# A fp32 two-block transformer stack on one core: taking the filler matmuls out of the norm transposes

## What is computed

```python
def swiglu(x, w_gate, w_up, w_down):
    return (jax.nn.silu(x @ w_gate) * (x @ w_up)) @ w_down
...
# first block, for layer in range(2)
f = swiglu(rms_norm(h, ffn1_pre_g[layer]), ...)
h = h + 0.5 * rms_norm(f, ffn1_post_g[layer])
hn = rms_norm(h, mix_pre_g[layer])
m = recurrent_block(hn, ...) if layer == 0 else forgetting_attention(hn, ...)
h = h + rms_norm(m, mix_post_g[layer])
f = swiglu(rms_norm(h, ffn2_pre_g[layer]), ...)
h = h + 0.5 * rms_norm(f, ffn2_post_g[layer])
...
# second block, for layer in range(4)
h = h + 0.5 * swiglu_2(rmsnorm(h, ffn_norm[layer, 0]), ...)
h = h + mix                              # gdn, short conv, nsa, gdn
h = h + 0.5 * swiglu_2(rmsnorm(h, ffn_norm[layer, 1]), ...)
```

## Time and profile before

| | |
|---|---|
| median of three runs | 3331.31 us |
| lowest and highest run | 3329.32 and 3336.26 us |
| the profiled execution, its own time | 3333.94 us |
| its span, first to last instruction | 3331.9 us |
| mean granted TensorE clock | 0.985 |
| TensorE (PE) busy | 3228.4 us, 97% |
| weight loads (PEld) busy | 2725.3 us, 82% |
| VectorE (DVE) busy | 1844.8 us, 55% |
| ScalarE (ACT) busy | 1561.7 us, 47% |
| DMA | 537 MB at 161 GB/s |

### The profile page before, as it was taken

One profiled execution on the slowest core, in us unless ns is written; L12 is line 12 of the kernel. 1 busy time (PEld: TensorE's weight loads), 2 busy tenths in 40 slices (PEclk: granted clock), 3 DMA queues, 4 the chain that ended last, 5 costly groups with the idle time before them and its releaser, 6 DMA issues.

```text
span 3331.9 us, 48269 instructions
## 1 busy us (share of the span) xinstructions
PE 3228.4 (97%) x18934; PEld 2725.3 (82%) x18934; DVE 1844.8 (55%) x2023; ACT 1561.7 (47%) x1896; POOL 187.4 (6%) x187
## 2 busy tenths in 40 slices
PE   7999999999999999989999999999999999999899
PEld 6878888887788889978888978888767888898787
DVE  4467556545545557555554655554655455475544
ACT  4446544444544446454454444444545444464543
POOL 0000001000000300300000000000410000003000
PEclk8999999999999999999999999999989999999999
DMA  7543554555255654225555555565513556551354
GB/s 228 189 149 121 183 189 159 182 186 168 95 189 164 193 186 153 78 91 192 187 184 189 169 164 186 173 195 189 158 52 114 185 173 197 177 159 60 115 188 139
DMA packets 415536, 537.14 MB, mean 161 GB/s; under 512 B 22956, under 2 KB 361084, under 8 KB 415152
## 3 DMA queue, kind: packets, MB, share of 16 engines
q1 hardware_dynamic: 413612, 528.76, 49.2%
q0 software_dynamic: 1792, 6.49, 0.8%
HBM read 534.13 MB, written 1.05 MB: 161 GB/s over the span
## 4 chain that ended last, share of the span: by engine, by line
PE 90%; DVE 4%; ACT 4%; DMA 1%; issue 1%; SPq 0%; ACTq 0%; DVEq 0%
PE banks L133 24%; PE banks L135 24%; PE banks L134 24%; PE banks L130 3%; PE banks L131 3%; PE banks L132 3%; PE banks L318 2%; PE banks L1891 1%; DVE w_lo L114 1%; ACT w_hi L106 1%; DMA raw<-ffn_w_up 1%; PE banks L253 1%; PE banks L1274 1%; PE banks L1003 1%; PE banks L1286 1%
## 5 line engine op out<-in xcount | busy, mean ns | idle before, releaser
L114 DVE TENSOR_TENSOR w_lo<-raw,w_hi 128x2048 fp32r<-128x2048 f32 x508 | 1169.6, 2307 | 663.6 <-ACT w_hi L106 663.5
L106 ACT ACTIVATE w_hi<-raw 128x2048 fp32r<-128x2048 f32 x508 | 970.6, 1916 | 509.5 <-PE banks L135 423.4
L133 PE MATMUL banks<-w_hi,xT_hi 128*128 128x512 f32 (+2 forms) x2588 | 1011.8, 391 | 38.8 <-DVE w_lo L114 14.6
L135 PE MATMUL banks<-w_hi,xT_lo 128*128 128x512 f32 (+2 forms) x2588 | 998.1, 386 | 0.0
L134 PE MATMUL banks<-w_lo,xT_hi 128*128 128x512 f32 (+2 forms) x2588 | 996.4, 385 | 0.0
L133 PEld LDWEIGHTS banks<-w_hi,xT_hi 128*128 128x128 f32 (+1 forms) x2588 | 491.1, 190 | 139.6 <-DVE w_lo L114 19.6
L135 PEld LDWEIGHTS banks<-w_hi,xT_lo 128*128 128x128 f32 (+1 forms) x2588 | 490.3, 189 | 98.0
L134 PEld LDWEIGHTS banks<-w_lo,xT_hi 128*128 128x128 f32 (+1 forms) x2588 | 491.4, 190 | 92.2
L133 PE MATMUL banks<-w_hi,hidT_hi 128*128 128x512 f32 x1056 | 411.9, 390 | 0.0
L135 PE MATMUL banks<-w_hi,hidT_lo 128*128 128x512 f32 x1056 | 411.1, 389 | 0.0
L134 PE MATMUL banks<-w_lo,hidT_hi 128*128 128x512 f32 x1056 | 410.9, 389 | 0.0
(11 more groups left out here) (431 smaller groups left out, 2423.5 us busy)
## 6 DMA issues: line engine op xcount, KB each, us to landing
raw<-ffn_w_gate_up SPq DMA_DIRECT2D x352, 512.0 KB
raw<-ffn_w_down SPq DMA_DIRECT2D x264, 512.0 KB
raw<-ffn_w_gate SPq DMA_DIRECT2D x88, 512.0 KB
raw<-ffn_w_up SPq DMA_DIRECT2D x88, 512.0 KB
raw<-gdn_w_in SPq DMA_DIRECT2D x64, 512.0 KB
raw<-sc_w_in SPq DMA_DIRECT2D x24, 512.0 KB
raw<-nsa_w_in SPq DMA_DIRECT2D x20, 512.0 KB
raw<-rg_w_in SPq DMA_DIRECT2D x20, 504.0 KB
```

The costliest lines, as they stand in the source:

```text
L106: c.nc.scalar.activation(c.w_hi[r][:], c.raw[r][:], ACT.Copy).then_inc(c.sem("w_hi_split"), 1)
L114: c.nc.vector.tensor_tensor(c.w_lo[r][:], c.raw[r][:], c.w_hi[r][:].bitcast(F32), ALU.subtract).then_inc(c.sem("w_lo_split"), 1)
L133: mm(out, x_hi, w_hi, start=start, stop=False)
L135: return mm(out, x_lo, w_hi, start=False, stop=stop)
```

## The change

The constant and the three lines of the loop are taken out. Nothing else differs: every other instruction of TensorE stands in the same order, and those of the other engines are the same. The bf16 identity and masks are still made at the start of the kernel and are used elsewhere.

```diff
@@ -233,7 +233,6 @@
         dve_rstd(c, dve, st)
 
 
-BUSY_MATMULS = 14
 
 
 def pe_norm(c, pe, st):
@@ -241,9 +240,6 @@
     if n == 0:
         pe.wait_ge(c.sem("masks_made"), MASK_STEPS)
     src = c.h if st.kind == "ffn" else c.xn
-    if n and (st.kind != "ffn" or st.source.post is not None and not st.keeps_h):
-        for _ in range(BUSY_MATMULS if st.source.post is None else 2 * BUSY_MATMULS):
-            c.nc.tensor.matmul(c.bank[NORM_BANKS[1]][:, 0:3 * P], c.ident_bf[:], c.causal_bf[:], start=True, stop=True)
     for m, t in PARTS:
         if st.kind == "ffn":
             wait_for_h(c, pe, st, m, t)
```

## The result

| | before | the change |
|---|---|---|
| median of nine runs | 3332.45 us | 3340.99 us |
| lowest and highest | 3328.98 and 3336.26 us | 3334.85 and 3344.24 us |
| ratio, 95% interval | | 1.0026 (1.0015 to 1.0036) |
| profiled execution, its time | 3333.94 us | 3339.73 us |
| its span, mean granted clock | 3331.9 us, 0.985 | 3337.2 us, 0.980 |

The change makes the kernel slower by 8.5 us, 5 to 12 by the interval. The time lies in my range; the size of the loss is 1.8 times my +4.7.

The account below looks back on a forecast made before the run. TensorE, busy for 97% of the span, was taken to bound the kernel. The terms 3.2 + 1.2 + 1.1 - 0.8 = +4.7 us on the 3331.3 us median gave 3336.0 us, range 3329.5 to 3343.0.

Parts of the forecast that it names:

- the fillers' own 36 us: All 224 fillers on TensorE take 36 us, not to be booked as gain, since TensorE would otherwise wait for the norm.
- Case 1: Ahead of the second block's four mixers: bare idle of 3.46 us likely drops the clock; +3.2 us, bounds 0 and 7.2.
- rival A: At stage starts: half clock is paid in full, half of each stretch; +11.4 us, 3342.7 us; chance 0.22.
- Case 2: Ahead of rg, kv and fa: the clock falls anyway, its half-clock stretch only lengthens; +1.2 us, bounds 0 and 1.5.
- Case 3: Behind fa, ahead of an FFN: 5.2 us of idle brings a new clock fall; +1.1 us, bounds 0 and 2.1.
- Case 4: Behind rg and ahead of the second block's first FFN: late fillers gone, -2.6, clock falls, +1.8; together -0.8 us.
- Rival B: Idle stretches below some 3.5 us do not bring the clock down; -0.3 us, 3331.0 us; chance 0.18.
- Rival C: Fillers hold no clock worth having, only the late ones count; -2.6 us, 3328.7 us; chance 0.05.

Follow-up runs that it names:

- e11: e10 without the fillers ahead of the four mixers of the second block; 3318.84 us, 0.9961 of before.
- e6: The change plus fillers at the longest waits inside the mixer stages, one rg group misplaced behind its wait; 3333.63 us, 1.0009 of before.
- e4: The change with 28 fillers put back ahead of each of the three FFNs; 3336.02 us, 1.0019 of before.
- the second pair: Second profiles of the change and of the kernel before, both unaltered; 3334.88 and 3333.56 us.
- e8: The kernel before, unaltered, run once more for a second profile; 3333.56 us.
- e2: The kernel before with 42 fillers in place of 28 behind rg and ahead of the second block's first FFN; 3338.05 us, 1.0020.
- e12: e10 with before's filler counts (14 and 28) at the ten starts in place of the fitted ones; 3319.16 us, 0.9963 of before.
- e1: The change with the 14 fillers put back ahead of each of the second block's four mixers; 3332.40 us, 1.0004 of before.
- e3: The kernel before with filler counts at the ten starts fitted to the wait lengths (44, 20, 16, 31); 3330.70 us, 0.9997.
- e9: e3 plus fillers at the longest waits inside the mixer stages and at the two first-slab waits; 3318.13 us, 0.9958 of before.
- e10: e9 plus 17 fillers at the 2.9 us wait in each gdn stage; 3313.77 us, 0.9944 of before.

## Why the prediction came out as it did

**What bounds the kernel, and the fillers' own 36 us.** Right. TensorE's busy time fell by 26 us and nothing was gained by it. The waits for xn did not move: 3.30 us of idle at the mixers.

**Case 1, the four mixers, +3.2 us.** The start price is right: 3.9 us in the profile of the change, 2.9 us in e11 and 3.4 in e6. All four fell in both profiles of the change and in e11, three of four in e4 and in e6. The first gdn start cost 1.76 us because its half clock lasted 5.6 us from the restart, where I had 3.6. My sign for rival A, a ninth k-tile over 1.3 us late, came true there, at one of the four places. It was a poor sign, since a longer stretch gives it as well: my own price, 0.72 us for 3.2 us and 0.38 for each further one, makes 1.6 us of 5.6, where A's makes 2.8.

**What the sum left out.** It has a term for the ten starts alone and none for the inside of a stage. No wait inside a stage grew by more than 0.02 us, which was my sign for that, but the half clock behind the waits changed. In the first pair of profiles the parts behind the starts add 1.5 us in the first gdn stage, 2.2 in the second and 2.1 in nsa, and take off 3.3 in rg and 1.5 in fa. With 4.9 us at the starts and some tenths elsewhere this is the 5.3 us by which the spans differ. It is not the 8.5 us of the medians, and the second pair, 1.2 us apart, is further from them. So the 4.7 agree with what was measured at the starts, and 3.6 us of the median loss have no place that the runs show.

**Case 2, rg, kv and fa, +1.2 us.** 1.6 us in the profile, just above my bound of 1.5, though not by one size: -0.1, 0.7 and 1.1. The half clock lasted 3.0, 5.0 and 5.6 us from the restart where I had 4.2 for all. I took it that the clock falls there anyway. In before, e8, e2 and e12, which all have 28 fillers there, eight of the twelve starts fell. So the typical run of before pays less than the profiled one, and the loss against the median is larger than against the profile.

**Case 3, behind fa, +1.1 us.** +0.64 us in both profiles of the change, with a stretch of 3.4 us in place of my 4.2; 1.6 us in e1 and in e6, where it lasted over 5. The first product came 0.5 us later, where I had asked for 0.6.

**Case 4, the late fillers, -0.8 us.** Right in its two terms, -1.3 us in the profile: fallen starts lost 0.6 to 0.9 us of the 1.3 they gained, where I had taken 0.9. e2 and e3 show the lateness by itself, +2.3 and -1.3 us a place.

**Rival A.** As a price of the start it fell: 2.8 to 3.4 us at 0.50 cost 0.6 to 0.9 us in every profile, and 5.0 to 6.0 us ahead of kv and the mixers cost 1.4 to 1.9 (against e3, which has none), not half of the stretch. By its time, 3342.7, it came nearer to the median than my forecast, but for a reason it did not have. The rule of the Trainium skill, page "TensorE: Matmul & The Clock Gate", section "Terms", that throttled time costs the missing share of the clock, can be put beside the whole runs. Nine runs of the change have a mean clock of 0.979 and 33 of before 0.987, so 2 x 0.008 x 3340 = 53 us more at half clock, and the rule makes 27 us of it. The runs show 8.5 us, or 11 if the 2.6 us of the late fillers are added back: about 0.2 us per us. The first pair of profiles has 37 us more at half clock, for 5.3 us of span, or 7.9 with the late fillers added back, which is again 0.1 to 0.2. The rest lies under waits for the other engines or is idle time itself. Inside one kernel the slope is steeper: among the nine runs of the change it is about 0.35 us per us, an estimate fitted to clocks of three digits, which is above the 0.33 from which A was to decide. So the small price is shown for the starts and for the pairs, not for every half-clock stretch; the one behind the 2.9 us wait of e9 took 1.5 us for 3.4. I had the mean clock falling by 0.004, from 28 us; the profiles have 0.005 and the runs 0.008.

**Rival B.** Fell: bare waits of 3.3 us brought the clock down at 18 of 20 starts. **Rival C** fell with it.

**The chances.** I gave 0.65 to within 0.2% and 0.32 to slower; it came out slower than that, by a little. That the time lies in the range owes something to rival A, which set its upper end by a price that the starts do not have. I made the sum against one profile of before that had a fall at all three of its uncertain starts, and knew it to lie above the median.

**What stays open.** What sets how long the half clock lasts behind an inner wait, and whether the change makes it longer in all or only moves it about. In the second gdn stage the long ones come with a fallen start in three of three profiles, in the first gdn stage also without one, and in rg the change went with less. I did not vary the time of a start by itself, and a few profiles cannot tell a rule from chance here. Open are also the 3.6 us above, and the 4 us by which e3's median stays behind its starts.

## What to carry to other kernels

Matmuls without use that stand in front of a wait can hold TensorE's clock. They are worth it when they start as the wait starts, end as it ends and stand ahead of the waiting instruction: here too few left 1.0 to 2.75 us uncovered, too many delayed the stage one for one, and a group behind the wait cost its whole 5 us. Look for all idle stretches of TensorE of some 2.7 us and more, not only those at stage boundaries (in fa the clock fell behind one of 1.6 us as well, in five of fourteen profiles, before and e10 among them); filling the ones inside the stages and at the start brought 17 us (e3 to e10, 3330.7 to 3313.8), where fitting the boundaries was worth 5 (e12 against e10) or, with the other waits open, 1 (e3 against before). And since falls come by chance, price a change of this kind by the mean clock over many runs and place by place in several profiles, not by one pair.

## What I had not expected of the hardware

What a wait costs in clock is not fixed by the wait. Behind the same 5.7 us wait of the same code the half clock lasted 3 us in some profiles and over 9 in others, and behind the 2.9 us wait anything from 0 to 6; with these two a gdn stage moves between 215.9 and 218.2 us. When fillers at the starts are taken out, these inner stretches change as well, up in the second gdn stage and down in rg, so a change can cost or gain time in places that it does not touch. And a run's time follows its clock closely: in the nine runs of the change the fastest, 3334.85 us, has a mean clock of 0.981 and the three slowest, 3343.8 to 3344.2 us, 0.977 to 0.978.
